# Router logits with tokens on partitions, row picks ahead of gates and counts, norm epsilon inside the square sum

## The reference

```python
def rmsnorm(x, g):
    y = x * rsqrt(mean(x * x, axis=-1) + 1e-6)
    return y * g

for l in (0, 1):
    x = x + hybrid_mixer(rmsnorm(x, norm_mix[l]), ...)      # mLSTM heads and S5 channels
    hn = rmsnorm(x, norm_ffn[l])
    x = x + (swiglu(hn, ...) if l == 0 else moe(hn, ...))
return rmsnorm(x, norm_final)

def moe(xt, w_router, b_router, w_gate, w_up, w_down):      # 8 experts, 2 for each token
    logits = xt @ w_router + b_router                        # (256, 8)
    top_v, top_i = top_k(logits, 2)
    gates = softmax(top_v)
    combine = einsum(gates, one_hot(top_i))                  # (256, 8)
    for e in range(8):
        out += combine[:, e:e+1] * ((silu(xt @ w_gate[e]) * (xt @ w_up[e])) @ w_down[e])
```

## Time and profile before

| | us |
|---|---|
| three runs | 1465.71, 1456.69, 1463.04 |
| median | 1463.04 |
| the profiled execution | 1457.26 |
| its span | 1455.1 |
| PE busy, of the span | 1341.7 (92%) |
| DVE busy | 470.8 (32%) |
| ACT busy | 278.4 (19%) |
| POOL busy | 98.5 (7%) |

### The profile page before, as it was taken

The page is one execution under the profiler, slowest core; times in us unless marked ns, Lnnn a source line. Parts: engine busy times, 40 slices in busy tenths (PEclk is TensorE's granted clock), DMA queues, the critical chain, the costliest instruction groups (busy, mean ns, idle before and its releaser), DMA issues.

```text
span 1455.1 us, 18657 instructions
## 1 busy us (share of the span) xinstructions
PE 1341.7 (92%) x7760; PEld 758.9 (52%) x7760; DVE 470.8 (32%) x1049; ACT 278.4 (19%) x515; POOL 98.5 (7%) x115
## 2 busy tenths in 40 slices
PE   6988899999799878999999999999999999987775
PEld 5845489999685535544455444444433344332322
DVE  7995965555589533041010100100110100000002
ACT  2541344443254100000011010001101101000001
POOL 4530000000442000000000000000000000000000
PEclk9999999999999989999999999999999999999999
DMA  9533345436221248799999959889999999999994
GB/s 286 153 116 116 115 164 185 174 116 244 75 87 59 101 191 332 250 363 414 413 411 416 411 213 410 338 353 401 410 411 416 410 410 416 410 412 415 410 414 199
DMA packets 126734, 423.50 MB, mean 291 GB/s; under 512 B 21632, under 2 KB 23864, under 8 KB 118456
## 3 DMA queue, kind: packets, MB, share of 16 engines
q1 hardware_dynamic: 121464, 421.75, 74.2%
q10 hardware_dynamic: 5184, 0.52, 0.4%
HBM read 421.20 MB, written 1.05 MB: 290 GB/s over the span
## 4 chain that ended last, share of the span: by engine, by line
PE 74%; DMA 14%; DVE 8%; issue 1%; SPq 1%; ACT 1%; POOL 0%; DVEq 0%; ACTq 0%
PE psall L2279 13%; DMA m_ring<-in_moe_w_down_dram 12%; PE psall L2370 11%; PE psall L2293 8%; PE psall L2308 6%; PE psall L1992 4%; PE psall L2381 3%; PE psall L2210 3%; PE psall L2090 3%; PE psall L2212 3%; PE psall L2211 3%; PE psall L2157 2%; PE psall L2256 2%; PE psall L2343 2%; PE psall L2409 2%; PE psall L2192 1%
## 5 line engine op out<-in xcount | busy, mean ns | idle before, releaser
L2293 PE MATMUL psall<-m_ring,xeT 128*64 128x448 f32 x1024 | 202.6, 543 | 22.5 <-DMA m_ring<-in_moe_w_up_dram 21.5
L2370 PE MATMUL psall<-m_ring,hidT 128*64 128x512 f32 (+1 forms) x672 | 201.0, 597 | 17.2 <-DMA m_ring<-in_moe_w_down_dram 16.4
L2279 PE MATMUL psall<-m_ring,xeT 128*128 128x448 f32 x512 | 195.7, 543 | 0.8 <-DVE xeT L1857 0.8
L2293 PEld LDWEIGHTS psall<-m_ring,xeT 128*64 128x64 f32 x1024 | 73.6, 137 | 139.9 <-issue 138.8
L2279 PEld LDWEIGHTS psall<-m_ring,xeT 128*128 128x128 f32 x512 | 97.3, 191 | 94.1 <-issue 92.9
L2370 PEld LDWEIGHTS psall<-m_ring,hidT 128*64 128x64 f32 (+1 forms) x672 | 72.6, 154 | 136.3 <-issue 120.1
L1879 DVE TENSOR_TENSOR hid<-e_silu,psall 64x448 f32<-64x448 f32 x32 | 19.9, 623 | 354.6 <-ACT e_silu L1231 352.5
L1577 DVE TENSOR_TENSOR w_lo<-ring,w_hi 128x1024 fp32r<-128x1024 f32 x66 | 80.5, 1225 | 68.0 <-ACT w_hi L1185 67.9
L2308 PE MATMUL psall<-m_ring,xeT 128*32 128x448 f32 x1024 | 102.0, 542 | 0.0
L2210 PE MATMUL psall<-hnT_hi,w_hi 128*128 128x256 f32 x352 | 99.6, 283 | 1.4 <-DVE hnT_lo L1715 1.4
L2212 PE MATMUL psall<-hnT_hi,w_lo 128*128 128x256 f32 x352 | 99.5, 283 | 0.0
(11 more groups left out here) (326 smaller groups left out, 1473.3 us busy)
## 6 DMA issues: line engine op xcount, KB each, us to landing
m_ring<-in_moe_w_gate_dram SPq DMA_DIRECT2D x128, 896.0 KB, 19.9
m_ring<-in_moe_w_up_dram SPq DMA_DIRECT2D x128, 896.0 KB, 17.1
m_ring<-in_moe_w_down_dram SPq DMA_DIRECT2D x64, 1792.0 KB, 19.1
ring<-in_w_in_dram SPq DMA_DIRECT2D x10, 2048.0 KB, 13.0
ring<-in_ffn_w_gate_dram SPq DMA_DIRECT2D x5, 2048.0 KB, 10.5
ring<-in_ffn_w_up_dram SPq DMA_DIRECT2D x5, 2048.0 KB, 7.7
ring<-in_ffn_w_down_dram SPq DMA_DIRECT2D x5, 2048.0 KB, 8.0
ring<-in_w_out_dram SPq DMA_DIRECT2D x4, 2048.0 KB, 7.9
```

The lines of the kernel that those rows point to most:

```text
L2279: ins = M(m_bank(key)[:, 0:MH], x[:, i, 0:P], weights(kind, i, s), start=(i == 0), stop=(i == KT - 1))
L2293: ins = M(m_bank(key)[64 * n:64 * n + 64, 0:MH], x[:, i, 0:64], weights(kind, i, s), start=(i == 0), stop=(i == KT - 1))
L2370: ins = M(y, hidT[:, r, 0:shape[0]], rows(r, 512 * n, 512), **ends)
```

## The change

Five things are altered.

1. **Norms.** Epsilon is no longer added by an instruction of its own: the square sum starts from `DM * EPS` instead of 0, the division by the number of channels is dropped, and the root of that number comes back as a constant factor where the result is used: in L1322 as a second operation, for the heads in the constants of the output gate, for the final norm in `gfin`, which is multiplied by it during the experts' second pair of items (one DVE instruction of 128x1024).
2. **Router logits.** `hnT` is now the stationary operand and the router's weights move (16 matmuls of 8 columns), so the output has tokens on partitions at once. The copy by ACT and the two transposes are gone. The first token tile's matmuls wait for each of the four pieces of `hnT` in turn instead of for all of them.
3. **Order on DVE.** The constants and the clearing of `pickg` stand ahead of the router's result. After the mask DVE goes on to places and to the row picks of item 0 (`choose_rows`); gates, counts and `choose_gates` follow behind `take_tokens(0)`.
4. **Counts** are a product of their own, behind the places.
5. **First gate-up matmuls of an item** wait for each gathered piece where they need it, not for the last piece before the first matmul.

The diff, without most of its unchanged lines:

```diff
@@ -432,9 +432,9 @@
         else:
-            out.append((("logits",), "A", 5))
             out.append((("router",), "V", 4))
             out.append((("pos",), "V", 5))
+            out.append((("counts",), "V", 6))
     return out
@@ -1212,8 +1212,6 @@
                             ffn_high(n)
-            arrived(act, ("logits",))
-            nc.scalar.activation(logitsT[0:NE, :], bank(("logits",))[0:NE, 0:SEQ], ACT.Copy).then_inc(drained["A"], 1)
             act.wait_ge(route_in, 1)
             nc.scalar.activation(rt[:, 8, :, 0:1], rt[:, 7, :, 0:1], ACT.Exp).then_inc(route_exp, 1)
@@ -1308,10 +1306,9 @@
-                link(V.tensor_tensor_reduce(out=scratch, in0=x_res[:, t, :], in1=x_res[:, t, :], scale=1.0,
-                                            scalar=0.0, op0=ALU.mult, op1=ALU.add, accum_out=small[:, t:t + 1]))
-                V.tensor_scalar(small[:, t:t + 1], small[:, t:t + 1], 1.0 / DM, EPS, ALU.mult,
-                                ALU.add).then_inc(ms_ready, 1)
+                V.tensor_tensor_reduce(out=scratch, in0=x_res[:, t, :], in1=x_res[:, t, :], scale=1.0,
+                                       scalar=DM * EPS, op0=ALU.mult, op1=ALU.add,
+                                       accum_out=small[:, t:t + 1]).then_inc(ms_ready, 1)
@@ -1319,7 +1316,7 @@
                     dve.wait_ge(rs_ready, before + t + 1)
-                    V.tensor_scalar(hn[:, t, :], x_res[:, t, :], small[:, t:t + 1], None,
+                    V.tensor_scalar(hn[:, t, :], x_res[:, t, :], small[:, t:t + 1], math.sqrt(DM), ALU.mult,
                                     ALU.mult).then_inc(hn_ready, 1)
@@ -1560,7 +1557,7 @@
                     ins = V.tensor_tensor_reduce(out=heads_sq[:, t * P:(t + 1) * P], in0=hm[:, t, h, :],
-                                                 in1=hm[:, t, h, :], scale=1.0, scalar=0.0, op0=ALU.mult,
+                                                 in1=hm[:, t, h, :], scale=1.0, scalar=DH * EPS, op0=ALU.mult,
                                                  op1=ALU.add, accum_out=small[:, 16 + t * NH + h:17 + t * NH + h])
                 return ins
@@ -1672,13 +1669,11 @@
                     wait_drained(dve, ("o", l, t))
-                    ins = V.tensor_scalar(o_gate[:, t, :], o_gate[:, t, :], 0.5, 0.5, ALU.mult, ALU.add)
+                    half = 0.5 * math.sqrt(DH)
+                    ins = V.tensor_scalar(o_gate[:, t, :], o_gate[:, t, :], half, half, ALU.mult, ALU.add)
                 link(ins)
                 out_s5(l, 0, 0)
-                link(head_out(l, NH - 1))
...
-                V.tensor_scalar(small[:, 16:16 + NT * NH], small[:, 16:16 + NT * NH], 1.0 / DH, EPS, ALU.mult,
-                                ALU.add).then_inc(ms_ready, 1)
+                head_out(l, NH - 1).then_inc(ms_ready, 1)
                 out_s5(l, 0, 1)
                 for t in range(NT):
@@ -1735,8 +1730,14 @@
             for e in range(NE):
-                ins = V.memset(desc[:, e:e + 1], float(NE - e))
+                V.memset(desc[:, e:e + 1], float(NE - e))
+            V.memset(want[:, :], 0.0)
+            for e in range(NI):
+                ins = V.memset(caps[:, e:e + 1], float(CAPS[e]))
             link(ins)
+            for rank, i in enumerate(ORDER):
+                V.memset(want[:, i - 1:i], float(rank))
+            link(V.memset(pickg[:, :, :], 0.0))
             dve.wait_ge(s_rt_in, 32)
             arrived(dve, ("router",))
             V.tensor_tensor(R(0), bank(("router",))[:, 0:NT * NE].rearrange("p (t e) -> p t e", t=NT), row(b_rt[:, :]),
@@ -1756,28 +1757,15 @@
             V.tensor_tensor(R(6), R(2), R(5), ALU.add).then_inc(route_mask, 1)
-            dve.wait_ge(route_exp, 1)
-            link(V.tensor_scalar(R1(9), R1(8), 1.0, None, ALU.add))
-            link(V.reciprocal(R1(9), R1(9)))
-            link(V.tensor_tensor(R1(10), R1(9), R1(8), ALU.mult))
-            V.tensor_tensor(R(11), R(2), wide(9), ALU.mult)
-            link(V.tensor_tensor(R(12), R(5), wide(10), ALU.mult))
-            link(V.tensor_tensor(R(11), R(11), R(12), ALU.add))
+            O = lambda i: over[:, i, :]
             arrived(dve, ("pos",))
             pos = bank(("pos",))
-            link(V.scalar_tensor_tensor(out=rt[:, 13, :, :].rearrange("p t e -> p (t e)"), in0=pos[:, 0:NT * NE], scalar=1.0,
-                                        in1=rt[:, 6, :, :].rearrange("p t e -> p (t e)"), op0=ALU.add, op1=ALU.mult))
-            V.tensor_scalar(R(13), R(13), 1.0, None, ALU.subtract)
-            O = lambda i: over[:, i, :]
-            V.tensor_copy(O(0), pos[:, NT * NE:NT * NE + NE]).then_inc(drained["V"], 1)
-            V.memset(want[:, :], 0.0)
-            for e in range(NI):
-                ins = V.memset(caps[:, e:e + 1], float(CAPS[e]))
-            link(ins)
-            for rank, i in enumerate(ORDER):
-                ins = V.memset(want[:, i - 1:i], float(rank))
-            V.tensor_copy(posI[:, :, 0:1], R(13)[:, :, 0:1])
-            link(V.tensor_copy(gateI[:, :, 0:1], R(11)[:, :, 0:1]))
+            V.scalar_tensor_tensor(out=rt[:, 13, :, :].rearrange("p t e -> p (t e)"), in0=pos[:, 0:NT * NE], scalar=1.0,
+                                   in1=rt[:, 6, :, :].rearrange("p t e -> p (t e)"), op0=ALU.add,
+                                   op1=ALU.mult).then_inc(drained["V"], 1)
+            wait_drained(dve, ("pos",))
+            link(V.tensor_scalar(R(13), R(13), 1.0, None, ALU.subtract))
+            link(V.tensor_copy(posI[:, :, 0:1], R(13)[:, :, 0:1]))
@@ -1832,18 +1820,40 @@
-            def choose(it, col):
+            def gates_of_tokens():
...
+                dve.wait_ge(route_exp, 1)
+                link(V.tensor_scalar(R1(9), R1(8), 1.0, None, ALU.add))
+                link(V.reciprocal(R1(9), R1(9)))
+                link(V.tensor_tensor(R1(10), R1(9), R1(8), ALU.mult))
+                V.tensor_tensor(R(11), R(2), wide(9), ALU.mult)
+                link(V.tensor_tensor(R(12), R(5), wide(10), ALU.mult))
+                link(V.tensor_tensor(R(11), R(11), R(12), ALU.add))
+                V.tensor_copy(gateI[:, :, 0:1], R(11)[:, :, 0:1])
+                arrived(dve, ("counts",))
+                V.tensor_copy(O(0), bank(("counts",))[:, 0:NE]).then_inc(drained["V"], 1)
+                wait_drained(dve, ("counts",))
...
+            def choose_rows(it, col):
...
                 for t in range(NT):
-                    p = posI[:, t, col]
-                    g = gateI[:, t, col]
-                    V.tensor_scalar(pick[:, t, first:first + n], times[:, 0:n], p, None, ALU.is_equal)
+                    ins = V.tensor_scalar(pick[:, t, first:first + n], times[:, 0:n], posI[:, t, col], None, ALU.is_equal)
+                ins.then_inc(v_pick, 1)
...
+            def choose_gates(it, col):
...
+                for t in range(NT):
                     for lo, hi, tile, base in experts.slots(it):
                         a = P * tile + base
-                        ins = V.tensor_scalar(pickg[:, t, a:a + hi - lo], times[:, lo:hi], p, g, ALU.is_equal, ALU.mult)
-                ins.then_inc(v_pick, 1)
+                        ins = V.tensor_scalar(pickg[:, t, a:a + hi - lo], times[:, lo:hi], posI[:, t, col],
+                                              gateI[:, t, col], ALU.is_equal, ALU.mult)
+                ins.then_inc(v_gate, 1)
...
+            def choose(it, col):
+                choose_rows(it, col)
+                choose_gates(it, col)
@@ -1888,9 +1898,10 @@
-            link(V.memset(pickg[:, :, :], 0.0))
-            choose(0, slice(0, 1))
+            choose_rows(0, slice(0, 1))
             take_tokens(0)
+            gates_of_tokens()
+            choose_gates(0, slice(0, 1))
             first_tiles()
             dve.wait_ge(ranks_ready, 1)
             choose(1, slice(1, 2))
@@ -1903,6 +1914,9 @@
                     second_tiles()
+                if pos == 2 and p == 1:
+                    dve.wait_ge(s_gfin, 16)
+                    link(V.tensor_scalar(gfin[:, :], gfin[:, :], math.sqrt(DM), None, ALU.mult))
                 if pos == 4 and p + 1 < NI // 2:
                     m_arrived(dve, ("pt", p))
                     for nxt in (2 * p + 2, 2 * p + 3):
@@ -2171,8 +2184,6 @@
                 norm(l, 1)
-                if l == 1:
-                    have_hnT(l, 1)
                 if l == 0:
                     within(1)
@@ -2219,25 +2230,24 @@
             pe.wait_ge(s_rt_in, 32)
-            open_bank(pe, ("logits",))
-            for k in range(KT):
-                ins = M(bank(("logits",))[0:NE, 0:SEQ], w_rt[:, k, :], hnT[:, k, :], start=(k == 0),
-                        stop=(k == KT - 1))
-            done(ins)
             open_bank(pe, ("router",))
-            wait_drained(pe, ("logits",))
             for t in range(NT):
-                ins = nc.tensor.transpose(bank(("router",))[:, t * NE:(t + 1) * NE],
-                                          logitsT[0:NE, t * P:(t + 1) * P], ident[0:NE, 0:NE])
```

(25 more changed lines are left out.)

6 lines of the change are left out of this document (4 added, 2 removed).

## The result

The changed kernel takes 1449.48 us in the median of 7 runs (1447.56 to 1451.73), the kernel before on the same chip 1458.96 us in 7 (1456.69 to 1465.71): ratio 0.9934, 95% interval 0.9918 to 0.9951. Two later comparisons of the two kernels gave 0.9959 (0.9944 to 0.9973) and 0.9945 (0.9928 to 0.9962). The mean of the three is 0.9946, that is 7.9 us less of 1458. The profiled execution took 1449.48 us, its span 1447.6.

The account below looks back on a forecast made before the run. PE's start of item 0, after a chain of PE, DVE and ACT, was taken to set the end. Terms 3.4 + 0.35 + 1.5 + 0.8 - 0.5 + 0.5 = 6.05 us less than 1460.15 gave 1454.1, range 1447 to 1463.

Parts of the forecast that it names:

- Rival A: Experts' work: the weight stream is the bound and absorbs PE's earlier start, leaving only the norms' gain; 1459.6 us, chance 0.15.
- Logits: Router logits: narrow matmuls start before the last `hnT` piece, so DVE's bias addition comes earlier; -3.4 us (-1.7 to -3.9).
- Constants, `n_list`, the second operation: DVE's constants, the later `n_list` with SP's load 0.9 us late, and L1322's second operation: each was to cost nothing.
- rival B: Norm scaling: a second operation loses the fast rate, 0.5 us more per scaling, 3 us in all; 1457 us, chance 0.06.
- Places: Mask to places: DVE waits for three matmuls instead of five and computes no gates meanwhile; -0.35 us (+0.2 to -0.5).
- Picks: Places to gather: three dependent steps and two picks instead of a memset and four picks; -1.5 us (-1.2 to -1.6).
- First expert matmul: Start of item 0: PE no longer waits for the second gathered piece; -0.8 us.
- Clock of the gather: Item 0's gather: PE at 0.50 from the norm into it, rising somewhere inside; +0.5 us (-1.5 to +1.4).
- Rival C: Item 0's first gate-up matmuls: PE stays at clock 0.50, 448-column records take 0.75 us; 1463.5 us, chance 0.05.
- Norms: Norms: the removed epsilon instruction saves 0.1 to 0.2 us in each of four; -0.5 us (0 to -1).
- rival D: Before item 0: only part of the shift, by low clock in gather or slow logit records; 1457 us, chance 0.14.
- the part that I took as fixed: From item 0's start to the end of the span: the distance was to stay 896.3 us.

Follow-up runs that it names:

- kernel with four dummies ahead of the mask: Changed kernel plus unread 256-column matmuls on PE: 8 before layer 1's second transposes, 4 before the mask wait, 2 before item 0's gather; 1445.41 us, ratio 0.9909.

## Why the prediction was right, and where it was not

The range of 1447 to 1463 holds the 1449.48 us, and the sign and the class (within 1%) are right. The forecast of 1454.1 is 4.6 us above the measurement: its base of 1460.15 stood 1.2 us over the median that the kernel before has in the same comparison (1458.96), and that comparison gave 9.5 us instead of 6.05. The mean of three comparisons, 7.9 us, is the better figure for the change. The mechanism is right for a part of it: item 0 starts 3.6 us earlier against the transposes, and the end moves with it. The other 4.3 us lie where the forecast had half a microsecond. Point by point:

- **What bounds it.** Shown in the main: PE's start of item 0. Delaying it by 10.35 us costs 7.7 us by the ratios and about 9 by the traces, and starting it 3.4 us earlier than the changed kernel does costs nothing later on. Rival A, which has all of a shift absorbed, is false. A part of it is true beyond the change's own size: with item 0 5.9 us earlier, PE waits 2 to 3 us more for weights.
- **Logits: the term of the sum that was mis-sized.** I took 0.13 us a record and 20 records behind the last piece of `hnT`, -3.4 us. At the low clock a record takes 0.213 us, and 27 of them stood behind it: -0.86 us. I had the right upper bound of 0.22 us, from records of 128 columns of weights and 128 moving, and set it aside because only 8 columns move here. The rows already showed how little the moving columns count: at the full clock a record takes 0.11 us with 8 of them and 0.13 us with 128. The Trainium skill (TensorE: Matmul & The Clock Gate, section LDWEIGHTS) gives a load of 128 columns 0.107 us. The trace agrees at the full clock (0.114 us a record) and not at half of it (0.213); there the measurement decides.
- **Constants, `n_list`, the second operation.** Nothing, as forecast; rival B is false (0.75 us for `hn`).
- **Places.** +0.09 instead of -0.35: the six records left run at the low clock, which was the upper bound's case.
- **Picks.** -1.49 against -1.5; undone alone, +1.15.
- **First expert matmul.** -0.94 against -0.8; undone alone, the 0.78 us wait returns.
- **Clock of the gather.** The forecast of PE at 0.50 from the norm into the gather was right: it is at 0.50 from 531.9 to 552.4 us without a break, where the kernel before had it full from 542.6 to 549.4. But the rise came 3.2 us into the gather instead of 4, and the 20 records behind it took 2.00 us: -0.42, not +0.5. Rival C is false; the first gate-up matmuls run at the full clock. The reason that I gave, a low stretch behind the gather of item 1, is weak: that stretch stands in only one of the three traces of the changed kernel.
- **Norms.** 0.19 us in layer 1's second norm and 0.27 in the last, in size as forecast. The 1.67 us by which the transposes start earlier is more than they can give; that start varied from 531.88 to 534.60 us among three traces of one kernel, and with the old norms back it was 533.22. The cause of the 1.67 us is not shown.
- **The rest.** Item 0 starts 3.62 us earlier against the transposes, not 5.55. Up to there it is rival D that happened, and by its own cause, the records at 0.22 us. The total came out near the forecast since the part that I took as fixed lost another 2.6 us, which the stretches of low clock that I had not counted can account for, and the transposes started 1.67 us earlier. These errors have opposite signs, so that the total came near is luck.

The kernel with four dummies ahead of the mask was the quickest of all: 1445.41 us, 5.3 below the changed kernel in the same comparison, with intervals of the ratios that overlap by 0.0007 (up to 0.9935, and from 0.9928).
